# Placing two large SBUF buffers ahead of the small ones in a four-layer decoder kernel

## The reference

```python
for i in range(DEPTH):                    # DEPTH = 4
    mixer = i % 3; j = i // 3
    h = rmsnorm(x, norm_mix[i])
    if mixer == 0:   y = hgrn2_mixer(h, a_w_in[j], lower_bounds[j], a_head_norm[j], a_w_out[j])
    elif mixer == 1: y = moba_mixer(h, b_w_qkv[j], b_w_out[j], rel_bias)
    else:            y = pool_mixer(h, c_w_group[j], c_scale[j])
    x = x + y
    x = x + sqrelu_mlp(rmsnorm(x, norm_mlp[i]), mlp_w1[i], mlp_w2[i])
return rmsnorm(x, norm_final)

def sqrelu_mlp(h, w1, w2):                # w1: 1024 x 4096, w2: 4096 x 1024
    a = jax.nn.relu(h @ w1)
    return (a * a) @ w2
```

## The kernel before, in words

| buffer | start, before | past a multiple of 64 |
|---|---|---|
| `raw`, `whi`, `wlo` | 16512, 49280, 82048 | 0 |
| `xT`, `hn`, `xhl` | 114816, 123008, 131200 | 0 |
| `rstd`, `ident`, `ones`, `gains`, `decay`, `masks`, `small`, `eps_col` | 147584 to 159488 | 0 |
| `rcol`, `flip`, `ident_r` | 159520, 159584, 160096 | 32 |
| `tab` | 159552 | 0 |
| `arena` | 160608 | 32 |
| `arena_r` | 211808 | 32 |

## Time and profile before

### The profile page before, as it was taken

How to read it: one execution, slowest core, us unless ns; L and a number is a source line. 1 busy time by engine, 2 the same in 40 slices (tenths; PEclk the granted TensorE clock), 3 DMA queues, 4 the chain that set the end, 5 groups by cost and what they waited for, 6 DMA issues and landing times.

```text
span 1240.5 us, 17170 instructions
## 1 busy us (share of the span) xinstructions
PE 1191.4 (96%) x6851; PEld 1037.3 (84%) x6851; DVE 792.3 (64%) x798; ACT 672.6 (54%) x793; POOL 47.7 (4%) x40
## 2 busy tenths in 40 slices
PE   6999899999999999999998899999988989999998
PEld 5999897888889989888886788888887988888886
DVE  6787756655656656755655875566778775655563
ACT  5955556444544444544455554455786555644543
POOL 4000000000001001000001100000100000000000
PEclk9999999999999999999999999999999999999999
DMA  9443234654455435555626455546434223555450
GB/s 346 151 136 102 97 108 170 207 200 167 171 206 185 144 114 166 178 200 180 217 96 222 149 204 200 207 139 208 142 122 136 103 93 113 170 203 204 148 207 34
DMA packets 85000, 202.90 MB, mean 164 GB/s; under 512 B 3293, under 2 KB 5415, under 8 KB 84688
## 3 DMA queue, kind: packets, MB, share of 16 engines
q1 hardware_dynamic: 84912, 202.10, 47.1%
q0 software_dynamic: 32, 0.02, 0.0%
HBM read 201.04 MB, written 1.06 MB: 163 GB/s over the span
## 4 chain that ended last, share of the span: by engine, by line
PE 80%; DVE 8%; ACT 6%; issue 3%; DMA 2%; POOL 0%; SPq 0%; ACTq 0%; DVEq 0%; POOLq 0%
PE acc L621 9%; PE acc L620 9%; PE acc L622 9%; PE misc L588 9%; PE hb L588 9%; PE misc L589 4%; PE hb L589 4%; PE hb L529 3%; PE hb L531 3%; PE hb L532 3%; DVE wlo L1349 3%; PE acc L724 2%; ACT whi L979 2%; PE hb L544 2%; PE hb L546 2%
## 5 line engine op out<-in xcount | busy, mean ns | idle before, releaser
L1349 DVE TENSOR_TENSOR wlo<-raw,whi 128x2048 fp32r<-128x2048 f32 x186 | 427.0, 2325 | 184.8 <-ACT whi L979 184.7
L979 ACT ACTIVATE whi<-raw 128x2048 fp32r<-128x2048 f32 x186 | 347.7, 1905 | 117.9 <-PE acc L622 101.5
L620 PE MATMUL acc<-whi,arena_r 128*128 128x512 f32 x512 | 202.6, 396 | 0.0
L621 PE MATMUL acc<-wlo,arena_r 128*128 128x512 f32 x512 | 202.3, 395 | 0.0
L622 PE MATMUL acc<-whi,arena_r 128*128 128x512 f32 x512 | 202.1, 395 | 0.0
L588 PE MATMUL hb<-xhl,whi 128*128 128x512 f32 x512 | 183.2, 400 | 5.3 <-DVE arena L1768 3.0
L588 PE MATMUL misc<-xhl,whi 128*128 128x512 f32 x512 | 182.9, 399 | 4.0 <-DVE arena L1750 2.0
L589 PE MATMUL misc<-xhl,wlo 128*128 128x256 f32 x512 | 143.7, 281 | 0.0
L589 PE MATMUL hb<-xhl,wlo 128*128 128x256 f32 x512 | 143.7, 281 | 0.0
L588 PEld LDWEIGHTS hb<-xhl,whi 128*128 128x128 f32 x512 | 96.2, 188 | 30.6 <-DVE arena L1768 3.8
L588 PEld LDWEIGHTS misc<-xhl,whi 128*128 128x128 f32 x512 | 96.2, 188 | 29.0 <-DVE arena L1750 2.3
(11 more groups left out here) (251 smaller groups left out, 1833.2 us busy)
## 6 DMA issues: line engine op xcount, KB each, us to landing
raw<-in_mlp_w_dram SPq DMA_DIRECT2D x128, 1024.0 KB, 5.4
raw<-in_a_w_in_dram SPq DMA_DIRECT2D x32, 1024.0 KB, 5.5
raw<-in_b_w_qkv_dram SPq DMA_DIRECT2D x12, 1024.0 KB, 7.5
raw<-in_a_w_out_dram SPq DMA_DIRECT2D x8, 1024.0 KB, 5.1
raw<-in_b_w_out_dram SPq DMA_DIRECT2D x4, 1024.0 KB, 5.1
arena<-in_x_dram SPq DMA_DIRECT2D x1, 1024.0 KB, 5.2
arena<-in_decay_dram SPq DMA_DIRECT2D x1, 1024.0 KB, 11.8
arena<-bias_rows SPq DMA_DIRECT2D x1, 1024.0 KB, 6.0
```

Of the source, the lines that this page charges most:

```text
L620: pe.matmul(o, ys, h, start=first and kt == 0, stop=False, skip_group_check=True)
L621: pe.matmul(o, ys, l, start=False, stop=False, skip_group_check=True)
L979: act.activation(whi[:, g % 2, u, 0:n], raw[:, g % 2, u, 0:n], ACT.Copy).then_inc(hi_done, 1)
L1349: dve.tensor_tensor(wlo[:, g % 2, u, 0:n], raw[:, g % 2, u, 0:n], whi[:, g % 2, u, 0:n].bitcast(F32), ALU.subtract).then_inc(lo_done, 1)
```

## The change

The two `sb` lines of `arena` and `arena_r` move up, ahead of `rstd` and the other small buffers. Sizes, types, views and instructions stay, and so does the order of instructions on every engine.

```diff
@@ -174,6 +174,8 @@
         hn = sb("hn", [P, KT, SEQ])
         xhl = sb("xhl", [P, KT, 2, SEQ], F32R)
         xh, xl = xhl[:, :, 0, :], xhl[:, :, 1, :]
+        arena = sb("arena", [P, 12800])
+        arena_r = sb("arena_r", [P, 4096], F32R)
         rstd = sb("rstd", [P, SEQ])
         ident = sb("ident", [P, P])
         ones = sb("ones", [P, P])
@@ -186,8 +188,6 @@
         tab = sb("tab", [BUCKETS + 1, HEADS])
         flip = sb("flip", [P, P], F32R)
         ident_r = sb("ident_r", [P, P], F32R)
-        arena = sb("arena", [P, 12800])
-        arena_r = sb("arena_r", [P, 4096], F32R)
```

## The result

| | before | after |
|---|---|---|
| median, 5 runs each | 1243.08 us | 1235.9 us (1234.7 to 1236.49) |
| the profiled execution, its span | 1242.63, 1240.5 us | 1235.63, 1233.5 us |
| mean granted TensorE clock | 0.989 | 0.992 |

The ratio is 0.9943, with a 95% interval of 0.9928 to 0.9957: 7.2 us faster, where 8.7 were forecast. The page's busy times and its chain, to be held against the earlier trace rows: TensorE's matmuls are 8.3 us less busy, its weight loads 0.9, and no other engine changed by more than 0.4.

A forecast was written before the change was run, and what follows sets the result against it. TensorE, busy 96% of the span, was taken as the bound. From the 1243.08 us median, 10.1 less (step 1) and 1.4 more (step 2), with 0 for steps 3 and 4, gave 1234.4 us; range 1232 to 1238, wide range 1232.0 to 1244.2.

The forecast's parts named there:

- Step 1: MLP's second product (L620 to L622, arena_r stationary): 1504 steps each 6.7 ns shorter once aligned to 64 bytes, 10.1 us less.
- step 2: Products with 256 moving columns: output projections 0.9 us, L712 and L713 0.4, L939 0.1; together 1.4 us more.
- rival C: The change doesn't do what it says, as the true unit isn't 64 bytes: 1243.1 us; 0.29 together with A.
- The cover: Low halves of the weights for the next first product: slack falls from 1.4 to 1.1 us and covers the gain.
- the sign that the forecast had named: New idle time before L588, ended by the vector engine's L1349, would show TensorE gaining its 10 us and then waiting.
- Steps 3 and 4: Vector and scalar engine on arena and arena_r (bounds -0.25 and +0.25 us), and DMA into arena: each taken as 0.
- The rule on cachelines: Skill's rule against the gain: with 16-byte lines, 512 bytes are 32 lines either way, so the sum would be 0.
- A: The second product's longer step has another cause (height in partition, bank, loop): 1243.1 us, or 1244.5 with step 2; 0.29 with C.
- B: Alignment makes reads collide in the second product: each step 6.4 ns longer, 9.6 us plus 1.4, 1254 us; chance 0.07.

The follow-up runs named there:

- g4_x192: After's order with xhl alone moved up by 192 bytes; whi, wlo and arena_r keep their places. 1234.28 us, ratio 0.9933.
- g2_w128_r128: After's order with whi, wlo and arena_r moved to multiples of 256, xhl still 128 past one. 1233.67 us, ratio 0.992.
- g1_r128: After's order with arena_r alone moved up by 128 bytes, to a multiple of 256. 1241.69 us, ratio 0.9991.
- f2: After's order with whi and wlo moved up by 64 bytes; the pad also pushed arena_r 128 up and moved xhl. 1240.95 us, ratio 0.999.
- f4: After's order with the views of arena_r beginning 16 bytes into it, nothing else moved. 1242.22 us, ratio 1.0004.

## Why the prediction was right, and where it was not

**Step 1, the second product: right line, right end, wrong reason, and a term too large.** The forecast was 1504 x 6.7 = 10.1 us. The steady step came out as foretold, 226.7 ns, and so did the median record, 389. But the mean over a stage is 228.0: the first dozen steps behind a first product run at 232 on average. The chunk gave 0.25 us for 0.31, and 32 of them 8.0 us for 10.1. That is the mis-sized term: 2.1 us too much. The forecast was off by only 1.5 (8.7 for 7.2), because step 2, below, was too large as well and has the other sign. L544, the nearest row, had shown it: its stages begin slower too (in before, from 29.24 us, one step of 314 ns and then 11 at 231 on average, the rest at 226.7), but the rows that I priced from began in the middle of one.

The reason, that a row of 512 bytes covers eight 64-byte blocks or nine, is refuted by the runs with `arena_r` 64 and 128 further up, both multiples of 64, with steps of 233.4 and 232.3 ns. What counts is whether stationary and moving operand begin at the same place within 256 bytes. The change brought that about because both big buffers happen to land 128 past a multiple of 256, where `whi` and `wlo` are. The forecast had noted the coincidence under rival C ("any unit up to 512 is served") and treated it as a safeguard; it was in fact what saved it, and that was luck. Had the pad between the buffers been 64 bytes larger, the same reasoning would have forecast the same gain in the second product, and there would have been none.

**The cover: right but for one place.** After's longest waits of TensorE are those of before, and the one of L588's matmul for L1349 is 0.5 us in both. But the slack of 1.1 us was read in one chunk, and the first product from 217.82 us has less. There a weight load of L588 waits for L1349 in after, which it doesn't in before. It is the sign that the forecast had named, at 0.28 us:

```profile
219.34 0.19 PEld L588 LDWEIGHTS hb<-xhl,whi 128*128 128x128 f32 x1 [0.28 <-DVE wlo L1349]
```

Who waited for whom, after, the whole span (us in total, times, longest):

```profile
PE hb L529 <- DVE arena L1481: 6.6, 2, 3.3
PE misc L650 <- DMA arena<-in_a_head_norm_dram: 6.6, 1, 6.6
PE acc L544 <- DVE wlo L1349: 4.9, 1, 4.9
PE acc L712 <- DVE arena L1473: 4.8, 1, 4.8
...
PE hb L588 <- DVE wlo L1349: 0.5, 1, 0.5
```

**Step 2, products with 256 columns: right in sign for two of three, and too large.** The projections with `arena_r` moving went from 118.3 to 120.0 ns (119.9 foretold): in layer 1, 136 steps in 16.32 us.

```profile
464.07 0.28 PE L531 MATMUL hb<-arena_r,whi 128*128 128x256 f32 x1
...
480.39 0.28 PE L532 MATMUL misc<-arena_r,wlo 128*128 128x256 f32 x1
```

Layer 1's gave back 0.31 us, 192 x 1.6. L939 went from 116.7 to 122 ns, (2.11 - 0.28) / 15:

```profile
680.30 2.11 PE L939 MATMUL misc<-whi,arena_r 128*128 128x256 f32 x16
```

L712 and L713, which had no row of their own, went the other way, from 119.1 to 117.7 on average inside their groups of eight. The 0.4 us forecast there is the one term with the wrong sign; the moving operand there is `decay`, not the weights. By the sizes of the buffers `decay` begins 192 past a multiple of 256 in both kernels, so that `arena_r` went from 96 below it to 64 below it, and never came in step. By these rows step 2 cost 0.9 - 0.4 + 0.2 = 0.7 us where 1.4 were forecast, and 8.0 less 0.7 is 7.3, against 7.2 measured.

**Steps 3 and 4: right.** DVE's L1773 and L1813 take 692 and 691 ns in after, ACT's L1118 takes 596 and 597, and the load of x lands after 5.1 us (5.2 before). The run that aligned `arena_r` alone had the gain of after within their intervals, so nothing is left for `arena` or its DMA to carry.

**The rule on cachelines.** "SBUF — State Buffer", section Specifications (TRN2), in the Trainium skill gives lines of 16 bytes. The runs agree with what it implies so far, that a place which is a multiple of 16 costs nothing by itself: the same `arena_r` at a multiple of 256 has 232.3 ns or 226.8, by where the weights are. That is no support for the zero it made of this change. "TensorE: Matmul & The Clock Gate", Part 2: What happens when you issue a matmul, has weight load and moving operand on ports of their own. The loads' medians of 187 and 188 ns in every layout agree; the 6.6 ns of the step, set by the place of one operand relative to the other, are an interaction that this rule doesn't foresee.

**The rivals.** A (another cause: height, bank, loop) is refuted by the pair of runs with 32 bytes of pad. Its observation, the 352.8 ns of an all-aligned pair where 346.4 were due, was sound and is a phenomenon of its own, below. B (two streams in step disturb each other) is refuted for 512 columns, where being in step is what makes them short. For 256 columns the rows lean its way, without a rule: 120.0 ns wherever the operands are in step, and shorter in most layouts where they aren't, but 120.0 again in some with 128 bytes between them. C didn't occur.

## What to carry to other kernels

Measure the distance from start to start of back-to-back matmuls, not their records; where two streams of the same shape differ by a few ns, compare where their two operands begin *relative to each other* before comparing their alignment. Here a step that went from 233.3 to 228.0 ns on average was worth 8 us over the 1504, and some bytes of padding are a cheap way to try it: move each operand alone, and check in the built program's addresses that nothing else moved with it. When a number agrees with a mechanism (16 columns, 64 bytes), find the placement for which that mechanism and its neighbours (128, 256, relative) part, before building on it.

## What the runs showed of the hardware

- A matmul of 512 moving float32 columns with a fresh weight load starts 226.7 ns after the last one, once the stream is steady, where stationary and moving operand begin at the same place within 256 bytes. It starts 232.3 to 233.3 ns after it where they are 16, 32, 64, 128 or 224 bytes apart (228.9 in the one case of `w_half` with 192; one stage with 16 bytes had 226.9).
- With 256 moving columns the step is 120.0 ns in step, and mostly shorter out of step. In layer 1's output projection it is 116.6 (16 apart) to 118.7 (128 apart). The shortest is an input projection of g4_x192, with `xhl` 192 above the weights within 256: 95 steps in 10.79 us, 113.6 ns. But with 128 between them that of g2_w128_r128 has 119.9 (41.35 to 52.74 us), and g1_r128, with 118.7 in layer 1, has 120.0 in layer 3.

```profile
40.64 0.28 PE L531 MATMUL hb<-xhl,whi 128*128 128x256 f32 x1
...
51.43 0.28 PE L534 MATMUL hb<-xhl,wlo 128*128 128x256 f32 x1
```

- The cadence keeps something from what ran before it. With only `arena_r` 64 bytes away, the first product, whose operands hadn't moved, ran at 346.9 ns a pair instead of 352.8 in every chunk but the first one or two of layers 0, 1 and 2. After's second product needs a dozen steps to reach 226.7 behind a first product in step, and none where `xhl` is 128 off. The two values of a chunk in f2, turn about, and the one short stage of f4 look like the same thing; what it hangs on isn't shown.

Open: what in the hardware makes 256 bytes the unit, why the cadence depends on what ran before, and whether a layout has both the pair of 346.9 and the step of 226.7, which would be some 0.25 us a chunk below after's (32 pairs x 5.9 ns = 0.19 us, and 0.06 us for the slow start). Neither the durations of the weight loads nor a wait tells these cases apart in these traces. Places off by less than 16 bytes weren't tried.
